# Modulation products with two k tiles of 512 outputs in a block: four column-group matmuls of 512 columns instead of sixteen of 128

## The chip, the cores and the metric

The kernel runs on one core of a Trainium2 chip (trn2). The metric is the device time of one execution in microseconds, as the median of several. The kernel uses five queues: TensorE (PE), VectorE (DVE), ScalarE (ACT), GpSimd (POOL) and SyncE (SP), which here only issues transfers.

## What is computed

Two blocks of two layers each. The first is a diffusion-style transformer block with adaptive modulation: an mLSTM and convolution mixer, then grouped attention, each followed by an MLP. The second has three attention branches. Only the modulation is touched here:

```python
silu_c = jax.nn.silu(c)          # (1, 1024)
silu_cc = jax.nn.silu(c_ctx)     # (1024,)
for layer in range(2):
    mod_x = jnp.split((silu_c @ ada_w[layer] + ada_b[layer])[:, None, :], 6, axis=-1)
    mod_c = jnp.split((silu_cc @ ada_w[layer] + ada_b[layer])[None, None, :], 6, axis=-1)
    hx = rms_norm(x, norm1_g[layer]) * (1 + mod_x[1]) + mod_x[0]
    ...
    x = x + mod_x[2] * y_x
    x = x + mod_x[5] * sqrelu_mlp(rms_norm(x, norm2_g[layer]) * (1 + mod_x[4]) + mod_x[3], ...)
```

`ada_w` is (2, 1024, 6144) in fp32: two vectors (c and c_ctx) times 12288 outputs, over 1024 inputs.

## The kernel before

**The modulation (ada).** `ada_w` is streamed as 96 blocks of 128 partitions x 1024 words (0.5 MB each). Two blocks are a pair; there are 48 pairs `q`. In the kernel before, a block holds 128 outputs with all eight k tiles of 128 inputs. `silu` holds, for each k tile, 32 columns of which two are the vectors and the rest zero. A matmul has `silu[:, k, :]` as the stationary operand (32 columns) and 128 outputs as the moving one, and writes 32 partitions of PSUM: k tile k goes to the column group k % 4, so the four groups of 32 partitions hold partial sums (`ada_products`, L1239 to L1261). The sum over the four groups, and the turn of the outputs from the free axis to partitions, are made by a second matmul in `ada_columns` (L1263 to L1270): VectorE first copies the bank to `ada_sum` (`sum_ada`, L2187), then TensorE multiplies each 128 outputs of it with `groups_to_rows`, a constant of two columns, and VectorE adds the bias and writes `mod` (`keep_ada`, L2193).

```python
for k in range(KT):
    rows = slice(32 * (k % 4), 32 * (k % 4) + 32)
    mm = pe.matmul(psum[rows, b, j * P:(j + 1) * P], silu[:, k, :], w[:, k, :], start=k < 4, stop=k >= 4)
```

**When.** The first eight pairs (16 blocks, `ADA_FIRST`) are computed at the start, since the first normalisation needs their outputs. Their blocks go through four slots of the tile `M`; SyncE loads block n when TensorE has read block n - 4 (L224 to L229), and behind the first four blocks it loads X (3 MB, both segments). VectorE adds up the squares of X between the pairs' sums (`ADA_SQUARES`, L2208 to L2216: k tiles 0 and 1 behind pair 1, and so on to pair 4). When all is done, `rms_stats` sums the squares on TensorE. The other 40 pairs are done at 40 points of the hybrid mixer's four heads, each behind a projection: `ada(point)` on TensorE (L1272) and on VectorE (L2201). Their blocks go through three slots of `stage`. In both programs a point has the columns of the pair before and then the products of its own pair; at the start the products of pair q come before the columns of pair q - 1.

**Queues.** Each engine runs its program in order. TensorE takes PSUM tiles from a ring of four banks (`Tiles.take`, waits `bank_free`); VectorE and ScalarE step through the same ring (`look`, `skip`) and wait for `tile_done`. `ada_tiles(point)` (L56) tells ScalarE how many tiles of the ring a point uses, so that it can skip them. The projections are matmuls in three terms (high and low parts of fp32r operands, L1111 to L1113, in `mm3`). ScalarE makes the high part of each weight block (L379), GpSimd the low part (L267).

Of the kernel before, what the change touches and what calls it, by code (L numbers as in the profile page):

```python
# [23 lines left out]
P = 128  # L24
D, KT = 1024, 8
# [8 lines left out]
ADA_BLOCKS = 2 * 6 * KT  # L34
# [21 lines left out]
def ada_tiles(point):  # L56


    q = ADA_FIRST // 2 + point
    return (point > 0 and q - 1 < ADA_BLOCKS // 2) + (q < ADA_BLOCKS // 2)  # L60

# [85 lines left out]
def build(nc, a, out, n_blocks, extra):  # L147
    with ExitStack() as ctx:  # L148
# [30 lines left out]
        silu = sb("silu", [P, KT, 32])  # L179
        ada_sum = sb("ada_sum", [P, 2, 2 * P])  # L180
        stage = sb("stage", [P, ADA_SLOTS, WORDS])
# [179 lines left out]
def act_program(nc, block, v, n_blocks, extra):  # L361
# [5 lines left out]
    def _(act):  # L367
# [130 lines left out]
        for k in range(KT):  # L498
            squares(k, ALL_SEGS)
        tiles.skip(ADA_FIRST)  # L500
        next_weights()
# [172 lines left out]
def attention_views(v):  # L674
# [6 lines left out]
    v_raw = M[:, 6 * SEQ:6 * SEQ + TOK]  # L681
    soft = v["ada_sum"][:, 0, :]
    root_q = [[soft[:, 20 + 16 * p + 8 * t:28 + 16 * p + 8 * t] for t in range(2)] for p in range(2)]
# [400 lines left out]
def pe_program(nc, block, v, n_blocks):  # L1084
# [6 lines left out]
    def _(pe):  # L1091
# [147 lines left out]
        def ada_products(q):  # L1239

            b = tiles.take(pe)
            for j in range(2):
# [5 lines left out]
                else:  # L1248
                    s = n % ADA_SLOTS
                    pe.wait_ge(v["stage_landed"][s], stage_landed[s].next(16))  # L1250
                    w = v["stage"][:, s]
                w = w.rearrange("p (k m) -> p k m", m=P)
                for k in range(KT):
                    rows = slice(32 * (k % 4), 32 * (k % 4) + 32)
                    mm = pe.matmul(psum[rows, b, j * P:(j + 1) * P], silu[:, k, :], w[:, k, :], start=k < 4, stop=k >= 4)
                if j == 0:
# [5 lines left out]

        def ada_columns(q):  # L1263

            b = tiles.take(pe)
            pe.wait_ge(v["ada_summed"], summed.next())
            for j in range(2):
                mm = pe.matmul(psum[:, b, 2 * j:2 * j + 2], ada_sum[:, q % 2, j * P:(j + 1) * P], v["groups_to_rows"],
                               start=True, stop=True)
            mm.then_inc(v["tile_done"], 1)  # L1270

        def ada(point):  # L1272

            if point > 0 and ADA_FIRST // 2 + point - 1 < ADA_BLOCKS // 2:
                ada_columns(ADA_FIRST // 2 + point - 1)
            if ADA_FIRST // 2 + point < ADA_BLOCKS // 2:
                ada_products(ADA_FIRST // 2 + point)

        for q in range(ADA_FIRST // 2):
            ada_products(q)  # L1280
            if q > 0:
                ada_columns(q - 1)
        ada_columns(ADA_FIRST // 2 - 1)

# [624 lines left out]
def dve_program(nc, block, v, a, out):  # L1909
# [7 lines left out]
    def _(dve):  # L1917
# [269 lines left out]
        def sum_ada(q):  # L2187
            b = look()
            cp(v["ada_sum"][:, q % 2, :], psum[:, b, 0:2 * P])
            free(b)  # L2190
            dve.sem_inc(v["ada_summed"], 1)

        def keep_ada(q):  # L2193
            b = look()
            i, m = q // 4, 2 * (q % 4)
            at = VEC["ada_b"] + 8 * i + m
            tt(mod[:, i, m:m + 2, :], psum[:, b, 0:4].rearrange("p (m c) -> p m c", c=2),
               vec[:, at:at + 2].unsqueeze(2).broadcast_to([P, 2, 2]), ALU.add)
            free(b)

        def ada(point):  # L2201
            if point > 0 and ADA_FIRST // 2 + point - 1 < ADA_BLOCKS // 2:
                keep_ada(ADA_FIRST // 2 + point - 1)
# [12 lines left out]
        keep_ada(ADA_FIRST // 2 - 1)  # L2216


# [1160 lines left out]
```

## Time and profile before

| | |
|---|---|
| median of 3 runs | 4305.46 us (4302.26, 4305.46, 4305.89) |
| span of the profiled execution | 4300.8 us (its own time isn't given apart; the span is 1.5 under the fastest run and 4.7 under the median) |
| TensorE matmul, weight load | 3983.3 us (93%), 3344.5 us (78%) |
| VectorE, ScalarE, GpSimd | 2080.8, 1500.1, 1648.3 us (48, 35, 38%) |
| ada products (L1255) | 1536 recorded passes, 7.5 to 473.4 us from the start |
| ada columns (L1268) | 192 recorded passes |

Matmul rows are passes, not matmuls: an fp32 matmul is recorded twice. A row's busy time covers its instructions from the first start to the last end, overlaps counted once, while "mean ns" is that of one, latency included; the distance from one start to the next tells the rate. Behind "idle before" stands what the engine last waited for; "DVEq L1972" is an event that VectorE's queue raised in line 1972. PEclk is the granted clock as a share of 2.4 GHz. ACT, DVE and POOL rows are single instructions on their engines.

### The profile page before, as it was taken

The page shows a single profiled execution, that of the slowest core. Times are in us where ns is not written, and L with a number is a line of the kernel's source. Part 1 is how long each engine was busy: PE and PEld are TensorE (multiplying, and loading weights), DVE is VectorE, ACT ScalarE, POOL GpSimd, SP SyncE. Part 2 cuts the span into 40 slices and gives each one's busy share as a digit, 9 for nine tenths or more (in the row PEclk, how much of TensorE's full clock was granted, in tenths as well). Part 3 has the DMA queues.
Part 4 walks back from the last instruction along what each step waited for, and adds up shares of the span by engine and source line. Part 5 has one row for each costly group of instructions (what it writes and reads, how often), then busy time and mean ns, then how long its engine had stood idle before and what let it go on. Part 6 is the DMA issues. An engine that isn't in the chain of part 4 may idle for free.

```text
span 4300.8 us, 62447 instructions
## 1 busy us (share of the span) xinstructions
PE 3983.3 (93%) x20764; PEld 3344.5 (78%) x20764; DVE 2080.8 (48%) x3374; ACT 1500.1 (35%) x2430; POOL 1648.3 (38%) x2044
## 2 busy tenths in 40 slices
PE   7899889999979889999899999899989999998997
PEld 6788779999967767887676778688866767887886
DVE  5655654322347764235737622532356475225225
ACT  2221221111235543222645633322245455333223
POOL 1111123333321115566243345465632433554655
PEclk7899989999989999999999999899989999999998
DMA  5333211111110002322121122233211211322222
GB/s 182 130 130 123 78 50 53 61 63 59 64 40 20 25 18 93 98 93 94 45 74 54 54 83 94 65 98 98 93 60 40 79 49 55 98 89 71 96 96 89
DMA packets 92774, 328.55 MB, mean 76 GB/s; under 512 B 10240, under 2 KB 12544, under 8 KB 92544
## 3 DMA queue, kind: packets, MB, share of 16 engines
q1 hardware_dynamic: 90928, 323.61, 22.8%
q8 instruction: 140, 2.29, 0.2%
q10 hardware_dynamic: 1616, 1.90, 0.1%
q14 instruction: 90, 0.74, 0.1%
HBM read 323.38 MB, written 2.10 MB: 76 GB/s over the span
## 4 chain that ended last, share of the span: by engine, by line
issue 65%; POOL 34%; POOLq 1%
POOL Wl L267 34%; POOLq L262 0%; POOLq L264 0%; POOLq L267 0%; POOLq L148 0%; POOLq L261 0%; POOLq L3371 0%
## 5 line engine op out<-in xcount | busy, mean ns | idle before, releaser
L267 POOL TENSOR_TENSOR Wl<-raw,Wh 128x256 fp32r<-128x256 f32 x2040 | 1648.1, 838 | 2651.9 <-ACT Wh L379 2651.7
L379 ACT ACTIVATE Wh<-raw 128x1024 fp32r<-128x1024 f32 x510 | 540.1, 1059 | 1748.8 <-PE psum L1113 1743.3
L1111 PE MATMUL psum<-Hh,Wh 128*128 128x512 f32 (+1 forms) x2704 | 1041.0, 385 | 72.6 <-DVEq L1972 24.7
L1112 PE MATMUL psum<-Hl,Wh 128*128 128x512 f32 (+1 forms) x2704 | 1015.9, 376 | 0.0
L1113 PE MATMUL psum<-Hh,Wl 128*128 128x512 f32 (+1 forms) x2704 | 1015.2, 375 | 0.0
L1111 PE MATMUL psum<-Gh,Wh 128*128 128x512 f32 (+3 forms) x2032 | 753.1, 371 | 27.3 <-DVEq L1972 16.3
L1113 PE MATMUL psum<-Gh,Wl 128*128 128x512 f32 (+3 forms) x2032 | 746.1, 367 | 0.0
L1112 PE MATMUL psum<-Gl,Wh 128*128 128x512 f32 (+3 forms) x2032 | 746.0, 367 | 0.0
L1111 PEld LDWEIGHTS psum<-Hh,Wh 128*128 128x128 f32 x2704 | 517.5, 191 | 198.8 <-issue 56.6
L1113 PEld LDWEIGHTS psum<-Hh,Wl 128*128 128x128 f32 x2704 | 517.3, 191 | 72.5
L1112 PEld LDWEIGHTS psum<-Hl,Wh 128*128 128x128 f32 x2704 | 518.6, 192 | 65.8 <-issue 1.9
L1111 PEld LDWEIGHTS psum<-Gh,Wh 128*128 128x128 f32 (+1 forms) x2032 | 383.7, 189 | 90.6 <-DVEq L1972 24.2
L1113 PEld LDWEIGHTS psum<-Gh,Wl 128*128 128x128 f32 (+1 forms) x2032 | 383.3, 189 | 51.9
L1112 PEld LDWEIGHTS psum<-Gl,Wh 128*128 128x128 f32 (+1 forms) x2032 | 383.9, 189 | 50.2 <-issue 1.1
L1929 DVE TENSOR_TENSOR hand<-hand 128x512 f32<-128x512 f32 (+1 forms) x160 | 111.8, 699 | 449.0 <-ACT hand L389 433.5
L2111 DVE SCALAR_TENSOR_TENSOR X<-psum,mod,X 128x256 f32<-128x256 f32 (+1 forms) x160 | 84.4, 548 | 375.1 <-PE psum L1113 374.6
L2107 DVE SCALAR_TENSOR_TENSOR X<-X,psum 128x512 f32<-128x512 f32 x64 | 44.0, 687 | 248.4 <-PE psum L1113 247.5
L2140 DVE TENSOR_TENSOR Gl<-hand,Gh 128x512 fp32r<-128x512 f32 (+1 forms) x160 | 155.5, 972 | 5.6
L1938 DVE CAST Gh<-hand 128x512 fp32r<-128x512 f32 (+1 forms) x160 | 117.7, 735 | 5.5
L1929 DVE TENSOR_TENSOR S<-psum,hand 128x512 f32<-128x512 f32 x32 | 22.1, 691 | 199.6 <-PE psum L1113 199.0
L923 ACT ACTIVATE stage<-psum,soft 128x512 f32<-128x512 f32 x128 | 86.5, 685 | 85.7 <-DVE soft L2959 85.6
L389 ACT ACTIVATE hand<-psum 128x512 f32<-128x512 f32 (+3 forms) x180 | 90.2, 525 | 9.6 <-DVEq L1975 9.6
(339 smaller groups left out, 4733.2 us busy)
## 6 DMA issues: line engine op xcount, KB each, us to landing
raw<-in_wstream SPq DMA_DIRECT2D x510, 512.0 KB, 3.4
stage<-in_ada SPq DMA_DIRECT2D x80, 512.0 KB, 4.2
M<-in_ada SPq DMA_DIRECT2D x16, 512.0 KB, 5.4
X<-in_xT SPq DMA_DIRECT2D x1, 2048.0 KB, 14.8
out<-X SPq DMA_DIRECT2D x8, 256.0 KB, 2.0
X<-in_ctxT SPq DMA_DIRECT2D x1, 1024.0 KB, 9.9
M<-in_memT ACTq DMA_DIRECT2D x1, 1024.0 KB, 5.3
M<-in_axial ACTq DMA_DIRECT2D x1, 512.0 KB, 3.6
```

What stands on the lines that cost most here:

```text
L267: last = pool.tensor_tensor(Wl[:, s, c], raw[:, s, c], Wh[:, s, c].bitcast(F32), ALU.subtract)
L379: act.activation(Wh[:, s], raw[:, s], ACT.Copy).then_inc(v["w_high"], 1)
L389: last = act.activation(hand[p, s, cols], one, func, **k)
L923: last = act.activation(stage[:, s, c * SEQ:(c + 1) * SEQ], psum[:, 4 + 2 * j + c, :], ACT.Exp, bias=soft[:, 4 * j + c:4 * j + c + 1], acc ...
L1111: pe.matmul(dst, a[0], b[0], start=first, stop=False)
L1112: pe.matmul(dst, a[0], b[1], start=False, stop=False)
L1113: return pe.matmul(dst, a[1], b[0], start=False, stop=last)
L1929: do(dve.tensor_tensor(dst, x, y, op))
L1938: do(dve.tensor_copy(dst, x))
L2107: last = dve.scalar_tensor_tensor(out=X[:, m, t0:t0 + n], in0=X[:, m, t0:t0 + n], scalar=1.0, in1=psum[:, b, 0:n], op0=ALU.mult, op1=ALU.add)
L2111: last = dve.scalar_tensor_tensor(out=X[:, m, lo:hi], in0=psum[:, b, lo - t0:hi - t0], scalar=mod[:, part, m, c:c + 1], in1=X[:, m, lo:hi] ...
L2140: do(dve.tensor_tensor(Gl[:, m, t0:t0 + w], r, Gh[:, m, t0:t0 + w].bitcast(F32), ALU.subtract))
```

## The change

A block now holds 512 outputs with two k tiles, so four blocks (two pairs) hold 512 outputs over all eight. Block j of pair q has the k tiles 4 (q % 2) + 2 j and the next, each of which goes to its own column group, as one matmul of 512 columns that fills the whole PSUM bank. VectorE copies the bank of an even pair to `ada_sum` (now one buffer of 512 columns, formerly two of 256) and adds the bank of the odd pair to it. The columns come once for two pairs, as four matmuls, and one bias instruction for 4 x 2 values. They stand before the products of the next even pair, at the start too. The points, the slots, the blocks' number and size, and the engines' other work are the same; the host packs the blocks in the new order.

```diff
-    return (point > 0 and q - 1 < ADA_BLOCKS // 2) + (q < ADA_BLOCKS // 2)
+    return len(ada_columns_at(point)) + (ADA_FIRST // 2 + point < ADA_BLOCKS // 2)
+
+
+def ada_columns_at(point):
...
     q = ADA_FIRST // 2 + point
+    return [q // 2 - 1] if point > 0 and q % 2 == 0 and q <= ADA_BLOCKS // 2 else []
...
-        ada_sum = sb("ada_sum", [P, 2, 2 * P])
+        ada_sum = sb("ada_sum", [P, 4 * P])
...
-                w = w.rearrange("p (k m) -> p k m", m=P)
-                for k in range(KT):
-                    rows = slice(32 * (k % 4), 32 * (k % 4) + 32)
-                    mm = pe.matmul(psum[rows, b, j * P:(j + 1) * P], silu[:, k, :], w[:, k, :], start=k < 4, stop=k >= 4)
+                w = w.rearrange("p (k m) -> p k m", m=4 * P)
+                for i in range(2):
+                    group = 2 * j + i
+                    k = 4 * (q % 2) + group
+                    mm = pe.matmul(psum[32 * group:32 * group + 32, b, :], silu[:, k, :], w[:, i, :], start=True, stop=True)
...
-            for j in range(2):
-                mm = pe.matmul(psum[:, b, 2 * j:2 * j + 2], ada_sum[:, q % 2, j * P:(j + 1) * P], v["groups_to_rows"],
+            for j in range(4):
+                mm = pe.matmul(psum[:, b, 2 * j:2 * j + 2], ada_sum[:, j * P:(j + 1) * P], v["groups_to_rows"],
                                start=True, stop=True)
...
         for q in range(ADA_FIRST // 2):
+            if q > 0 and q % 2 == 0:
+                ada_columns()
             ada_products(q)
-            if q > 0:
-                ada_columns(q - 1)
-        ada_columns(ADA_FIRST // 2 - 1)
+        ada_columns()
...
         def sum_ada(q):
             b = look()
-            cp(v["ada_sum"][:, q % 2, :], psum[:, b, 0:2 * P])
+            if q % 2 == 0:
+                cp(v["ada_sum"][:], psum[:, b, :])
+            else:
+                tt(v["ada_sum"][:], v["ada_sum"][:], psum[:, b, :], ALU.add)
+                dve.sem_inc(v["ada_summed"], 1)
             free(b)
-            dve.sem_inc(v["ada_summed"], 1)
...
         for q in range(ADA_FIRST // 2):
+            if q > 0 and q % 2 == 0:
+                keep_ada(q // 2 - 1)
             sum_ada(q)
-            if q > 0:
-                keep_ada(q - 1)
...
-    ada = w["ada_w"].reshape(2, KT, P, 6 * KT, P).transpose(0, 3, 2, 1, 4).reshape(ADA_BLOCKS, P, WORDS)
+    ada = w["ada_w"].reshape(2, KT // 2, 2, P, 12, 4 * P).transpose(0, 4, 1, 3, 2, 5).reshape(ADA_BLOCKS, P, WORDS)
```

The order on TensorE at the start, from the columns of the first outputs on, through pairs 2 and 3, first before the change (L1255 products, one pair is 16 matmuls; L1268 columns; `ada_landed` is a block's transfer, `ada_summed` VectorE's sum):

```order
L1268 MATMUL psum<-const,ada_sum 128x2 [waits ada_summed,bank_free2]
L1268 MATMUL psum<-const,ada_sum 128x2
L1255 MATMUL psum<-M,silu 32x128 [waits ada_landed0,bank_free3]
L1255 MATMUL psum<-M,silu 32x128 x7
L1255 MATMUL psum<-M,silu 32x128 [waits ada_landed1]
L1255 MATMUL psum<-M,silu 32x128 x7
L1268 MATMUL psum<-const,ada_sum 128x2 [waits ada_summed,bank_free0]
L1268 MATMUL psum<-const,ada_sum 128x2
L1255 MATMUL psum<-M,silu 32x128 [waits ada_landed2,bank_free1]
L1255 MATMUL psum<-M,silu 32x128 x7
L1255 MATMUL psum<-M,silu 32x128 [waits ada_landed3]
L1255 MATMUL psum<-M,silu 32x128 x7
```

And with the change (L1262 products, L1275 columns):

```order
L1275 MATMUL psum<-const,ada_sum 128x2 [waits ada_summed,bank_free2]
L1275 MATMUL psum<-const,ada_sum 128x2 x3
L1262 MATMUL psum<-M,silu 32x512 [waits ada_landed0,bank_free3]
L1262 MATMUL psum<-M,silu 32x512
L1262 MATMUL psum<-M,silu 32x512 [waits ada_landed1]
L1262 MATMUL psum<-M,silu 32x512
L1262 MATMUL psum<-M,silu 32x512 [waits ada_landed2,bank_free0]
L1262 MATMUL psum<-M,silu 32x512
L1262 MATMUL psum<-M,silu 32x512 [waits ada_landed3]
L1262 MATMUL psum<-M,silu 32x512
L1275 MATMUL psum<-const,ada_sum 128x2 [waits ada_summed,bank_free1]
L1275 MATMUL psum<-const,ada_sum 128x2 x3
```

Before, the sum waited for between two pairs was that of the pair ahead of the last one; now it is that of the last one, and comes after every second pair.

On VectorE at the same place, from the end of the squares of k tiles 0 and 1 (S sums the squares), before:

```order
L1938 COPY ada_sum<-psum 128x256 [waits v_chain,tile_done]
L1929 TENSOR_TENSOR mod<-psum,vec 128x4 [waits v_chain,tile_done]
L1929 TENSOR_TENSOR S<-S,hand 128x384 [waits v_chain,handed] x4
L1938 COPY ada_sum<-psum 128x256 [waits v_chain,tile_done]
L1929 TENSOR_TENSOR mod<-psum,vec 128x4 [waits v_chain,tile_done]
L1929 TENSOR_TENSOR S<-S,hand 128x384 [waits v_chain,handed] x4
```

And with the change:

```order
L1936 TENSOR_TENSOR mod<-psum,vec 128x8 [waits v_chain,tile_done]
L1945 COPY ada_sum<-psum 128x512 [waits v_chain,tile_done]
L1936 TENSOR_TENSOR S<-S,hand 128x384 [waits v_chain,handed] x4
L1936 TENSOR_TENSOR ada_sum<-ada_sum,psum 128x512 [waits v_chain,tile_done]
L1936 TENSOR_TENSOR S<-S,hand 128x384 [waits v_chain,handed] x4
```

The four additions of squares stood behind a sum whose columns were already in TensorE's queue behind another pair; now the second sum of a group stands behind them, with TensorE's columns waiting for it.

## Rows read from the trace of the kernel before

**Rows 1.** The page, part 1: busy time of the engines.

```profile
PE 3983.3 (93%) x20764; PEld 3344.5 (78%) x20764; DVE 2080.8 (48%) x3374; ACT 1500.1 (35%) x2430; POOL 1648.3 (38%) x2044
```

**Rows 2.** Timeline of TensorE, start: start us, us, operation, count, idle before.

```profile
20.48 2.27 PE L1255 MATMUL psum<-M,silu 128*32 128x128 f32 x32 [8.53 <-DMA M<-in_ada]
...
23.62 1.93 PE L1255 MATMUL psum<-M,silu 128*32 128x128 f32 x32
...
31.79 0.98 PE L1268 MATMUL psum<-const,ada_sum 128*128 128x2 f32 x4 [0.30 <-DVEq L2191]
...
38.58 1.87 PE L1268 MATMUL psum<-const,ada_sum 128*128 128x2 f32 x8
40.31 2.70 PE L1198 MATMUL psum<-const,S 128*128 128x1 f32 x12
```

**Rows 3.** Stretches: length, busy PE, PEld, DVE, ACT, POOL, clock, DMA, GB/s.

```profile
20.00:44.00 24.00, 21.37 (x233) 16.74 (x234) 13.28 (x32) 11.00 (x19) 4.06 (x6) 0.50 0.79 277
...
70.00:180.00 110.00, 98.50 (x812) 88.10 (x812) 61.51 (x132) 23.59 (x42) 15.42 (x20) 0.86 0.31 107
180.00:290.00 110.00, 99.39 (x861) 88.08 (x860) 68.58 (x123) 24.20 (x43) 16.61 (x22) 0.92 0.38 137
290.00:400.00 110.00, 97.53 (x856) 87.92 (x855) 68.87 (x120) 23.68 (x39) 17.49 (x23) 0.91 0.36 130
```

**Rows 4.** Waits of TensorE, 70 to 480 us: us in total, times, longest.

```profile
PE psum L1111 <- DVE Pl L2161: 18.4, 9, 5.3
...
PE psum L1111 <- DVEq L1965: 9.1, 5, 2.1
PE psum L1255 <- DVEq L1965: 1.6, 1, 1.6
```

**Rows 5.** Timeline of TensorE in narrow windows, and one group by source.

```profile
70.01 0.33 PE L1112 MATMUL psum<-Hl,Wh 128*128 128x384 f32 x1
70.18 0.34 PE L1113 MATMUL psum<-Hh,Wl 128*128 128x384 f32 x1
70.45 0.32 PE L1255 MATMUL psum<-stage,silu 128*32 128x128 f32 x4
...
70.45 0.75 PE L1255 MATMUL psum<-stage,silu 128*32 128x128 f32 x20
...
136.71 1.13 PE L1150 MATMUL psum<-M,tab 4*128 4x512 f32 x4
...
2281.68 1.02 PE L1150 MATMUL psum<-diag,const 128*128 128x512 f32 x2
...
L1150 PE MATMUL psum<-diag,const x28: 590/590/591, 2281.7 to 3623.8; 128*128 128x512 f32 x28
```

**Rows 6.** Timeline of TensorE's weight loads at the start.

```profile
21.67 0.63 PEld L1255 LDWEIGHTS psum<-M,silu 128*32 128x32 f32 x16 [0.56 <-DMA M<-in_ada]
```

**Rows 7.** Timeline of TensorE at a point of the hybrid stage.

```profile
78.93 0.58 PE L1268 MATMUL psum<-const,ada_sum 128*128 128x2 f32 x4 [0.89 <-DVEq L2191]
79.44 1.08 PE L1255 MATMUL psum<-stage,silu 128*32 128x128 f32 x32
80.45 0.33 PE L1111 MATMUL psum<-Wh,Hh 128*128 128x128 f32 x1
```

**Rows 8.** VectorE by form, 0 to 480 us: busy us, mean ns, idle before.

```profile
L1929 DVE TENSOR_TENSOR mod<-psum,vec 128x4 f32<-128x4 f32 x47 | 7.5, 160 | 39.0 <-PE psum L1268 35.8 <-DVE Vl L1929 0.9 <-PE psum L1255 0.7
...
L1929 DVE TENSOR_TENSOR tab<-psum,tab 128x512 f32<-128x512 f32 x6 | 4.1, 691 | 0.2
```

**Rows 9.** Timeline of VectorE at a point of the hybrid stage.

```profile
187.89 0.16 DVE L1929 TENSOR_TENSOR mod<-psum,vec 128x4 f32<-128x4 f32 x1
188.20 0.42 DVE L1938 COPY ada_sum<-psum 128x256 f32<-128x256 f32 x1 [0.15 <-DVE mod L1929]
188.87 3.35 DVE L2414 RECIPROCAL tab<-tab 128x512 f32<-128x512 f32 x1 [0.25 <-DVE ada_sum L1938]
```

**Rows 10.** Timeline of VectorE at the start: the squares of two k tiles.

```profile
24.04 2.67 DVE L1929 TENSOR_TENSOR S<-S,hand 128x384 f32<-128x384 f32 x4
```

More of the change, by code:

```diff
@@ L499, in _ @@
             squares(k, ALL_SEGS)
-        tiles.skip(ADA_FIRST)
+        tiles.skip(ADA_FIRST // 2 + ADA_FIRST // 4)
         next_weights()
@@ L681, in attention_views @@
     v_raw = M[:, 6 * SEQ:6 * SEQ + TOK]
-    soft = v["ada_sum"][:, 0, :]
+    soft = v["ada_sum"]
     root_q = [[soft[:, 20 + 16 * p + 8 * t:28 + 16 * p + 8 * t] for t in range(2)] for p in range(2)]
@@ L1261, in ada_products, with ada_columns @@
                     v["ada_read"].append((v["tile_done"], tiles.at))
-        def ada_columns(q):
+        def ada_columns():
             b = tiles.take(pe)
             pe.wait_ge(v["ada_summed"], summed.next())
-            for j in range(2):
-                mm = pe.matmul(psum[:, b, 2 * j:2 * j + 2], ada_sum[:, q % 2, j * P:(j + 1) * P], v["groups_to_rows"],
+            for j in range(4):
+                mm = pe.matmul(psum[:, b, 2 * j:2 * j + 2], ada_sum[:, j * P:(j + 1) * P], v["groups_to_rows"],
                                start=True, stop=True)
@@ L1272, in ada @@
         def ada(point):
-            if point > 0 and ADA_FIRST // 2 + point - 1 < ADA_BLOCKS // 2:
-                ada_columns(ADA_FIRST // 2 + point - 1)
+            for _ in ada_columns_at(point):
+                ada_columns()
             if ADA_FIRST // 2 + point < ADA_BLOCKS // 2:
@@ L1279, in _ @@
         for q in range(ADA_FIRST // 2):
+            if q > 0 and q % 2 == 0:
+                ada_columns()
             ada_products(q)
-            if q > 0:
-                ada_columns(q - 1)
-        ada_columns(ADA_FIRST // 2 - 1)
+        ada_columns()
         rms_stats(ALL_SEGS, 0)
@@ L2188, in sum_ada, with keep_ada @@
             b = look()
-            cp(v["ada_sum"][:, q % 2, :], psum[:, b, 0:2 * P])
+            if q % 2 == 0:
[3 more added lines that the diff above has]
+                dve.sem_inc(v["ada_summed"], 1)
             free(b)
-            dve.sem_inc(v["ada_summed"], 1)
-        def keep_ada(q):
+        def keep_ada(group):
             b = look()
-            i, m = q // 4, 2 * (q % 4)
+            i, m = group // 2, 4 * (group % 2)
             at = VEC["ada_b"] + 8 * i + m
-            tt(mod[:, i, m:m + 2, :], psum[:, b, 0:4].rearrange("p (m c) -> p m c", c=2),
-               vec[:, at:at + 2].unsqueeze(2).broadcast_to([P, 2, 2]), ALU.add)
+            tt(mod[:, i, m:m + 4, :], psum[:, b, 0:8].rearrange("p (m c) -> p m c", c=2),
+               vec[:, at:at + 4].unsqueeze(2).broadcast_to([P, 4, 2]), ALU.add)
             free(b)
         def ada(point):
-            if point > 0 and ADA_FIRST // 2 + point - 1 < ADA_BLOCKS // 2:
-                keep_ada(ADA_FIRST // 2 + point - 1)
+            for group in ada_columns_at(point):
+                keep_ada(group)
             if ADA_FIRST // 2 + point < ADA_BLOCKS // 2:
@@ L2215, in _ @@
         for_pe()
-        keep_ada(ADA_FIRST // 2 - 1)
+        keep_ada(ADA_FIRST // 4 - 1)
         dve.wait_ge(v["masks_loaded"], 16)
```

## The prediction

> **What bounds the kernel now.** I read the totals of the page first. TensorE is busy for 93% of the span [rows 1], so a microsecond on its queue counts wherever it isn't waiting. The modulation work (ada) lies wholly in the first 480 us of 4300.8: of its 48 pairs eight stand at the start and 40 in the hybrid stage, and a pair's 16 matmuls are recorded as 32 passes, so an fp32 matmul runs as two passes [rows 2]. Nothing after that changes, so the question is about two stretches.
>
> The first is the start, the first 40 us: TensorE works through eight pairs of blocks between block loads and VectorE's sums, at a granted clock of 0.50 of 2.4 GHz in 20 to 44 us, i.e. 1.2 GHz [rows 3]. The second is the hybrid mixer, 70 to 480 us, where 40 pairs are slipped between the projections. There TensorE is busy for about 90% of the time [rows 3]. The chief waits in that stretch are for VectorE: 18.4 us for the low parts of the probabilities (Pl, L2161) and 9.1 us for PSUM banks to be freed (L1965), with 1.6 us more of these at the ada matmuls, 10.7 in all [rows 4].
>
> How do the narrow ada matmuls run today? By windows of the timeline that end early, starting at 70.45: four passes cover 0.32 us, twenty cover 0.75 us [rows 5]. So four passes, one for each group of 32 columns, run side by side, and each of the four further waves adds 0.11 us. A pair has 32 passes, 8 waves. On the full array a 512-column fp32 matmul shows 1.02 us for its two passes [rows 5]; a single one is recorded at 0.59 us, so the second began 0.43 us after the first: 0.107 us per 128 columns. A wave of 128 columns at 0.11 us is therefore all streaming and nearly no fixed cost.
>
> **The change, part by part.**
>
> *Products.* Sixteen matmuls of 128 columns become four of 512, one per column group. Before: 8 waves x 0.11 = 0.88 us. Now: 2 waves x 0.43 = 0.86 us, if the four groups still run together. That is 0.02 us per pair, 0.8 us over 40 pairs at most. At 1.2 GHz both double: a pair took 1.93 us [rows 2] and will take the same. The number of columns per group (1024 passed per pair) hasn't changed; that is why the cut in instructions is worth so little.
> The Trainium skill ("TensorEngine Tiling (Array Packing)", section Instruction Overhead) says otherwise: about 60 cycles of overhead for each matmul. Its 60 cycles, 25 ns at 2.4 GHz, on each of six waves saved would be an estimated 0.15 us per pair and 6 us in all, and the sum below would end at 4304.7. The spacing of 0.11 against 0.107 us speaks against it.
>
> *Half-filled waves.* A block now holds two of the four groups, where it held all four. If the second block lands late, the first one's matmuls run with two groups idle, and the pair ends a full 2 x 0.85 us (1.2 GHz) after the second landing instead of 0.85. At the start block 5 lands 0.56 us late by the weight-load row at 21.67 [rows 6]. In the hybrid stage no wait for a block stands among the ada matmuls' waits [rows 4], since three slots are loaded ahead, so I cost it at nothing there.
>
> *Columns.* 48 groups of two matmuls become 24 of four, the same 96 matmuls. Warm, two take 0.51 us from start to start (78.93 to 79.44), products 1.01 (79.44 to 80.45) [rows 7]. Two points cost 2 x 1.52 = 3.04 us now, and 0.95 + 2 x 1.0 = 2.95 afterwards, to which the odd point adds a switch from the full array to 32-column groups that the columns used to cover (70.18 to 70.45 is 0.27 us where successive projection passes stand 0.17 apart [rows 5]): 0.1 us. So 3.05 against 3.04: TensorE's own work is unchanged.
>
> *VectorE.* 48 copies of 128x256 (0.42 us) become 24 copies and 24 additions of 128x512 from PSUM; the nearest row is an addition of 128x512 with one operand in PSUM, 0.691 us [rows 8]. 48 biases (0.160 us) become 24. With what lies around them, one point takes 187.89 to 188.87 = 0.98 us: 0.16 + 0.15, then 0.42 + 0.25 [rows 9]. Afterwards an even point takes 0.31 + 0.69 + 0.15 = 1.15 and an odd one 0.69 + 0.25 = 0.94, so two points 2.09 instead of 1.96. Over 20 such twos that is +2.6 us of VectorE time. VectorE alternates between waiting and being waited for; I take 1.0 us of it as on the path.
>
> *Fewer tiles.* 20 PSUM tiles fewer go through the ring of four banks in the hybrid stage, so TensorE can run further ahead. Bounds: nothing, or half of the 10.7 us of bank waits [rows 4]. Since VectorE holds the remaining ones longer, I take nothing.
>
> *The order at the start.* This is the term that matters. Before, the columns of pair q-1 stood behind the products of pair q, so the sum by VectorE had a whole pair to hide behind; even so TensorE waited 0.30 us at 31.79 [rows 2]. Now they stand ahead of the products of pairs 2, 4 and 6, and TensorE must wait for the sum of the pair that it has only just finished, with VectorE's squares (2.67 us for four additions) in between [rows 10]. Worked forward: X ends and block 4 lands as before (20.48 [rows 2]), block 5 at 21.67. Pair 2 ends at 21.67 + 1.71 + 0.2 = 23.6. VectorE sums it to 24.3 and does squares to 27.1, and only then sums pair 3 (done at 25.3): to 27.9. Columns of the first group start at 28.1 and take 1.73 (38.58 to 40.31 holds eight passes [rows 2]), to 29.9. Pair 4 runs to 31.8; VectorE: sum to 32.5, squares to 35.3, sum of pair 5 to 36.1. Columns 36.3 to 38.1, pair 6 to 40, pair 7 to 41.8 (its blocks were asked for from 31.6 on, so they are there), its sum to 42.5, four columns 42.75 to 44.5. The statistics, and all that follows, start at 44.5 instead of 40.31: **+4.2 us**. Bounds: if VectorE never held TensorE up, only the last links remain, 0.27 for the larger sum and 0.85 for columns that no longer overlap it: +1.1. If one more half-filled pair falls on the path, 6.
>
> Sum: +4.2 + 1.0 = +5.2 us. Against the execution profiled: 4300.8 + 5.2 = 4306.0 us of span. The median of the runs, 4305.46, stands 4.7 above that span (the launch around it and the spread of the runs), so **4310.7 us**.
>
> *Clock.* The mean granted clock of 0.86, 0.92 and 0.91 in 70 to 400 us means that some 68 us there (2 x 0.14 x 110, and so on) ran at 1.2 GHz [rows 3]. These stretches follow idle time of TensorE, which shifts by microseconds. A tenth more or less would be 3.4 us of time either way.
>
> **The rivals.** A measurement tells about 0.2% of this kernel from no change, 8.6 us: faster is under 4296.9, slower over 4314.1.
> 1. *The four groups no longer run together.* If passes of 512 columns overlap only two by two (each block brings two groups, with a wait between), a pair takes 4 x 0.43 = 1.71 us, 0.85 more: 34 us over 40 pairs, and some 10 at the start at half clock: 4355 us. It decides from 0.07 us more per pair. Against: two 512-column matmuls of 4 rows each, in different row tiles and with a wait each, took 1.13 us for all four passes at 136.71, hardly more than the 1.02 of one; and today's second block has its wait before the 17th pass, which the run of twenty passes crosses without a gap [rows 5]. 6 in 100.
> 2. *The start and the hybrid stage at their upper ends.* 6 + 2.6 + 3.4 = 12: 4317. It needs VectorE's additions on the path throughout; for it speaks that VectorE is what TensorE waits for [rows 4]. 18 in 100.
> 3. *Run-ahead pays.* All bank waits go (-10.7) and the clock gains 3.4, against +4.2 at the start: 4295.6, faster. For it: 20 tiles leave the ring. Against: those waits come where VectorE does reciprocals of 3.35 us [rows 9], which no ring of four hides. 7 in 100.
> 4. *A fixed cost per matmul* that the spacing hides: at most 6 us back, 4305, no change. 10 in 100.
>
> **How the numbers follow.** The forecast has 59 in 100. Within 0.2%: 0.59 + 0.10 = 0.69; slower: 0.18 + 0.06 = 0.24; faster: 0.07. The range takes in the unknown costs: low end 1.1 - 5.3 - 3.4 = -7.6, high end rival 2, +12, and a little beyond its middle: 4299 to 4319.
>
> **What would show it.** Right: passes of the products x8 in about 1.05 us warm; columns in groups of 8 passes, 24 of them; in 20 to 44 us TensorE waits for the sum's event (28, 36 and 42 us) and the statistics start near 44.5; VectorE additions of 128x512 into ada_sum at 0.69 us; the same gap of some 5 us at 480 us as at 70. Wrong: a pair over 1.2 us warm (rival 1), the statistics before 42 us (the start was not bound by VectorE), or a gap at 480 us that differs by more than 4 us from the gap at 70.

## The result, and the profile after

The changed kernel takes **4313.8 us** (median of 17 runs, 4307.96 to 4319.96), the kernel before, in runs alternating with it on the same chip, 4305.46 us (17 runs). The ratio is 1.0019, 95% interval 1.0013 to 1.0025: slower by 8.3 us. The forecast was 4310.7 in a range of 4299 to 4319, with "no change that can be measured" as the likeliest: by the forecast's own bound for a change, 8.6 us, the 8.3 still fall under it, though the interval leaves out 1. The execution profiled took 4309.77 us, 1.8 more than its span of 4308.0.

The page, part 1, of the changed kernel, against [rows 1]:

```profile
PE 3989.0 (93%) x19612; PEld 3310.2 (77%) x19612; DVE 2093.8 (49%) x3350; ACT 1501.4 (35%) x2430; POOL 1646.8 (38%) x2044
```

TensorE has 1152 passes less (48 pairs by 24) and 5.7 us *more* busy time, VectorE 13 us more. Cutting the number of passes saved nothing. A pair at full clock, and the projection pass that follows it (timeline of TensorE, hybrid stage; columns as in [rows 2]):

```profile
82.36 1.07 PE L1262 MATMUL psum<-stage,silu 128*32 128x512 f32 x8
83.36 0.33 PE L1117 MATMUL psum<-Wh,Hh 128*128 128x128 f32 x1
```

Start to start it is 1.00 us, where it was 1.01 [rows 7]. The four groups still run side by side.

The start, timeline of TensorE, against [rows 2]:

```profile
20.78 5.54 PE L1262 MATMUL psum<-M,silu 128*32 128x512 f32 x16 [6.05 <-DMA M<-in_ada]
28.47 1.02 PE L1275 MATMUL psum<-const,ada_sum 128*128 128x2 f32 x8 [2.16 <-DVEq L2200]
29.43 3.85 PE L1262 MATMUL psum<-M,silu 128*32 128x512 f32 x16
36.62 1.84 PE L1275 MATMUL psum<-const,ada_sum 128*128 128x2 f32 x8 [3.34 <-DVEq L2200]
38.38 4.15 PE L1262 MATMUL psum<-M,silu 128*32 128x512 f32 x16
43.47 1.02 PE L1275 MATMUL psum<-const,ada_sum 128*128 128x2 f32 x8 [0.94 <-DVEq L2200]
44.35 1.48 PE L1204 MATMUL psum<-const,S 128*128 128x1 f32 x12
...
53.65 0.66 PE L1117 MATMUL psum<-Hh,Wh 128*128 128x384 f32 x1 [4.15 <-DVEq L1979]
```

Columns stand at 28.5, 36.6 and 43.5 us, each behind a wait for VectorE's sum, and the statistics begin at 44.35 instead of 40.31. But they take 1.48 us, where they took 2.70: the first projection starts at 53.65, and before at

```profile
50.83 0.66 PE L1111 MATMUL psum<-Hh,Wh 128*128 128x384 f32 x1 [4.15 <-DVEq L1972]
```

so **2.8 us** of the 4.0 are left there. The stretches tell why, against [rows 3]:

```profile
20.00:44.00 24.00, 16.79 (x69) 5.55 (x70) 13.18 (x25) 9.59 (x17) 1.02 (x2) 0.66 0.78 275
44.00:70.00 26.00, 17.44 (x83) 14.70 (x83) 19.56 (x38) 11.24 (x20) 4.49 (x7) 0.87 0.27 104
70.00:180.00 110.00, 99.98 (x569) 82.84 (x567) 65.46 (x129) 24.18 (x43) 16.55 (x20) 0.86 0.30 106
180.00:290.00 110.00, 97.41 (x585) 79.30 (x585) 71.68 (x116) 23.87 (x40) 18.15 (x24) 0.92 0.38 134
290.00:400.00 110.00, 97.25 (x593) 79.85 (x592) 71.84 (x117) 22.55 (x38) 15.31 (x20) 0.91 0.37 130
400.00:490.00 90.00, 83.04 (x513) 68.82 (x512) 58.86 (x96) 19.92 (x35) 15.34 (x20) 0.94 0.35 123
```

The granted clock in 20 to 44 us is 0.66 of 2.4 GHz, where it was 0.50; in 44 to 70 us 0.87, where it was 0.79.

The end of the hybrid stage is told by the last columns, the last place of the modulation work. The row by tile (first and last start) of before, and of the changed kernel:

```profile
L1268 PE MATMUL psum<-const,ada_sum x160: 166/251/353, 78.9 to 480.2; 128*128 128x2 f32 x160
```

```profile
L1275 PE MATMUL psum<-const,ada_sum x160: 166/251/251, 94.1 to 490.0; 128*128 128x2 f32 x160
```

They stand **9.8 us** later, of which 2.8 came from the start: 7.0 us arose in the hybrid stage, where 1.0 was forecast. After that the gap stays between 9.3 and 10.6 us to 850 us, is 8.0 at 900, and 7.2 at the end (spans of 4308.0 and 4300.8). These 2.6 us came back where the work is the same, by less idle time of TensorE; what shortened it was not looked into. Waits of TensorE, 70 to 490 us, against [rows 4]:

```profile
PE psum L1117 <- DVE Pl L2168: 19.4, 9, 5.5
PE psum L1156 <- DVEq L1979: 11.2, 7, 2.2
PE psum L1117 <- DVEq L1972: 7.8, 5, 2.1
PE psum L1262 <- DVEq L1972: 3.3, 3, 1.1
```

In all 41.7 us. Before, the same view adds 9.6 (L1150) and 1.3 (L1268) to the rows shown, 40.0 in all. So the waits explain some 2 of the 7 us. The stage as a whole, from 70 us before and 72.8 after (the same place of the program) to the last columns, of before and of the changed kernel (columns as in [rows 3]):

```profile
70.00:480.20 410.20, 369.99 (x3199) 331.07 (x3198) 254.43 (x472) 88.45 (x153) 62.94 (x81) 0.91 0.36 126
```

```profile
72.80:490.00 417.20, 374.88 (x2239) 308.01 (x2238) 265.18 (x452) 88.89 (x154) 62.98 (x81) 0.91 0.35 124
```

TensorE is busy 4.9 us longer and idle 2.1 us longer. Laid over the stretches of granted clock in the two traces, its busy time at 1.2 GHz is 64.1 us, where it was 55.2. Work at 1.2 GHz takes about twice its time (a pair 1.93 us for 1.00), so half of the 8.9 us more, 4.5, is the clock's share. Of the 7.0 us, 4.5 are thus the clock, 2.1 waits and 0.4 TensorE's own work. The mean clock, 0.91 in both, hides this: it counts idle time too.

VectorE's work by form, 0 to 490 us:

```profile
L1945 DVE COPY ada_sum<-psum 128x512 f32<-128x512 f32 x24 | 16.6, 692 | 16.5 <-PE psum L1262 15.3 <-DVE mod L1936 0.9
L1936 DVE TENSOR_TENSOR ada_sum<-ada_sum,psum 128x512 f32<-128x512 f32 x24 | 16.5, 688 | 30.0 <-PE psum L1262 29.1
...
L1936 DVE TENSOR_TENSOR mod<-psum,vec 128x8 f32<-128x8 f32 x23 | 3.8, 167 | 20.0 <-PE psum L1275 18.9 <-DVE Vl L1936 0.5
```

These are the durations that the forecast took (0.69, 0.69, 0.16).

### The profile page after: what moved, and what is told of

Its sections match the earlier page's. It is cut to its first block, busy times and chain, and to the rows that moved or that the text cites. A ratio compares the mean times of both kernels' runs of the same rounds, so it can differ in the third digit from the quotient of the medians.

```text
span 4308.0 us, 60047 instructions
## 1 busy us (share of the span) xinstructions
PE 3989.0 (93%) x19612; PEld 3310.2 (77%) x19612; DVE 2093.8 (49%) x3350; ACT 1501.4 (35%) x2430; POOL 1646.8 (38%) x2044
## 4 chain that ended last, share of the span: by engine, by line
issue 65%; POOL 34%; POOLq 1%
POOL Wl L273 34%; POOLq L268 0%; POOLq L270 0%; POOLq L273 0%; POOLq L154 0%; POOLq L267 0%; POOLq L3381 0%
```

## The experiments

Three theories for the 7 us of the hybrid stage. **A**: VectorE's longer sums. **B**: the late start, which shifts everything behind it against the clock's stretches. **C**: TensorE's own order, that is the columns of two old pairs standing together at every second point.

All results first. "Start" is the gap to the kernel before at the first projection (50.83), "hybrid end" that at the last columns (480.2), both in the profiled execution; the median's difference is against the kernel before in the same set of runs (4304.7 to 4306.5). A gap is that of one execution against one, and both can lie off their kernel's median: the one of the kernel before took 4302.26 us, 3.2 under it, that of fill_pairs 6.6 over its own, that of new_start 5.0 under. Small differences between gaps need the medians beside them. The ratio is not quite the quotient of the medians; the fit further down goes by the ratios. Where an expectation counts blocks, they are the weight blocks as ScalarE rounds them: in the kernel before, block 9 is at 210 us, blocks 20 to 23 at 435 to 489.

| kernel | median | against before | ratio, 95% interval | start | hybrid end |
|---|---|---|---|---|---|
| the change | 4313.8 | +8.3 | 1.0019 (1.0013 to 1.0025) | 2.8 | 9.8 |
| old_start | 4312.54 | +7.1 | 1.0012 (1.0003 to 1.0021) | 1.2 | 10.4 |
| new_start | 4309.41 | +4.0 | 1.0011 (1.0002 to 1.0020) | 3.3 | 4.0 |
| late_3 | 4306.48 | +1.1 | 1.0006 (0.9998 to 1.0015) | 4.9 | 3.4 |
| short_sums | 4305.3 | -0.1 | 0.9998 (0.9989 to 1.0007) | 3.1 | 1.2 |
| wide_copies | 4317.41 | +12.7 | 1.0030 (1.0019 to 1.0041) | 0.0 | 12.7 |
| squares_moved | 4308.5 | +3.8 | 1.0010 (1.0001 to 1.0019) | 0.6 | 10.1 |
| products_first | 4312.52 | +7.8 | 1.0014 (1.0005 to 1.0023) | 2.7 | 12.3 |
| same_load | 4310.68 | +4.5 | 1.0017 (1.0008 to 1.0026) | 1.2 | 10.2 |
| two_pairs | 4307.64 | +1.4 | 1.0004 (0.9995 to 1.0013) | -0.1 | 6.2 |
| fill_change | 4312.66 | +6.2 | 1.0016 (1.0007 to 1.0026) | 2.2 | 9.4 |
| fill_pairs | 4306.51 | 0.0 | 1.0002 (0.9993 to 1.0011) | 1.5 | 8.1 |
| odd_points | 4341.75 | +35.3 | 1.0085 (1.0071 to 1.0099) | 1.2 | 40.0 |

### Which half costs: old_start and new_start

The first has the start of the kernel before (its blocks, order and sums for the first 16 blocks) and the hybrid stage of the change; the second the reverse. In old_start:

```
-        for q in range(ADA_FIRST // 2):
-            if q > 0 and q % 2 == 0:
-                ada_columns()
-            ada_products(q)
-        ada_columns()
+        for q in range(ADA_FIRST // 2):
+            ada_products(q)
+            if q > 0:
+                ada_columns_old(q - 1)
+        ada_columns_old(ADA_FIRST // 2 - 1)
```

> The start (the first eight pairs, their block layout, sums and columns) as in the kernel before, the hybrid stage's 40 pairs as in the change. If the two parts add up, the start returns its 3 us (the statistics at 40.3 us instead of 44.4 in the trace) and what is left is the hybrid stage's own share. Theory A (the hybrid form itself costs, through VectorE's sums or through more stretches at 1.2 GHz): about 5 to 6 us over the kernel before, so 4311. Theory B (the late start shifts TensorE against the chip's clock decisions, and that made the rest): back to the kernel before within 2 us, 4305 to 4307.

> The start as in the change, the hybrid stage's 40 pairs as in the kernel before. Theory A: 3 us over the kernel before, 4308.5, and the distance between the two traces stays at 3 us through the hybrid stage. Theory B: the whole 8 us, 4313, with the distance growing in the hybrid stage.

Both halves cost: 1.0012 and 1.0011, which add up to the 1.0019 of the whole within their intervals. In new_start the gap stays between 3.9 and 5.0 us from 66 to 700 us, but for 6 us near 77 where it touches 5.9; nothing is added in an unchanged hybrid stage. In old_start the hybrid stage adds 9 us to a start that is 1.2 late.

### Is it only that everything is late: late_3

The kernel before, with one reciprocal of 512 columns more on VectorE ahead of the statistics:

```
+        do(dve.reciprocal(diag.rearrange("p b q -> p (b q)"), const_cols))
```

> The kernel before with one more reciprocal of 512 columns on VectorE (3.35 us, into a tile that nothing reads then) before it lets TensorE start the statistics. A pure delay of about 3 us at 40 us. Theory A: 3 us over the kernel before, 4308.5. Theory B: as the change, 4313, since only the delay matters.

The gap is 4.9 us at the first projection and 3.4 at the last columns, and the median is within the interval of no change. Theory B falls: a late start alone doesn't come out larger at the end of the stage.

### VectorE's sums: short_sums and wide_copies

The change with sums of 128 columns in the hybrid stage (it leaves out three quarters of the hybrid stage's sums, so most of the modulation):

```
-                cp(v["ada_sum"][:], psum[:, b, :])
+                cp(v["ada_sum"][:, cols], psum[:, b, cols])
```

> The change, but in the hybrid stage VectorE copies and adds only the first 128 of the 512 columns (the others keep their sums of the start, so most of the modulation there is left out): 0.29 us instead of 0.69 for each of 40 sums, 16 us less work for VectorE. If VectorE's longer sums made the hybrid stage's share, it goes, and some more: 4308 or less. If it is the clock through something else, the time stays at 4312 to 4314.

And the kernel before with each copy of the hybrid stage done twice:

```
             cp(v["ada_sum"][:, q % 2, :], psum[:, b, 0:2 * P])
+            if q >= ADA_FIRST // 2:
+                cp(v["ada_sum"][:, q % 2, :], psum[:, b, 0:2 * P])
```

> The kernel before, in which VectorE does each copy of a pair's sum in the hybrid stage twice: 0.42 us more per point, 40 points, about 17 us more work of VectorE with nothing else moved. It measures how much of VectorE's added work comes out as time. Theory A (VectorE's longer operations carry the hybrid share of the change, because VectorE is late at its reciprocals): half of it or more shows, 8 to 17 us at 490 us, so 4313 to 4322. Theory C (the hybrid share comes from TensorE's side, the order of its wide passes and columns, and VectorE has room): the gap at 490 us stays under 4 us and the time at or under 4309. Late in the hybrid stage the gap then either stays or shrinks with the clock, by some 3 us.

The two copies are recorded at 0.88 us where one took 0.42 [rows 9]: 0.46 us more at 40 points, 18.4 in all, of which 12.7 come out: **0.7 us for each us of VectorE's work** in this stage. Short sums take 16 us off VectorE (40 sums of 0.69 down to 0.29), and the gap at the hybrid end falls by 8.6 us. So VectorE's time matters here, and Theory A looked proven. It wasn't: the change adds only 2.6 us of such work, worth 1.8. The price was right and the quantity too small by far; that sent me to the next pair.

### The same VectorE load, TensorE's order kept: same_load and two_pairs

same_load is the change with copies of 384 columns (it leaves out a quarter of what they copy), so that two points cost VectorE what they cost before:

```
+            n = 4 * P if q < ADA_FIRST // 2 else 3 * P
             if q % 2 == 0:
-                cp(v["ada_sum"][:], psum[:, b, :])
+                cp(v["ada_sum"][:, 0:n], psum[:, b, 0:n])
```

> The change, in which the copies of the hybrid stage carry 384 of the 512 columns (it leaves out a quarter of what they copy, so a part of the modulation). A copy then takes some 0.56 instead of 0.69 us, and two points hold VectorE for 1.96 us, exactly as in the kernel before: what is left of the change in the hybrid stage is TensorE's order of work, its wide passes and its tiles. Theory A (VectorE's 2.6 us of added work carry the hybrid share): the gap to the kernel before at 490 us falls from 9.8 us (the change) to 3 to 4.5 us, and the median comes to 4306 to 4309. Theory A', by the slope of 0.6 to 0.7 us per us of VectorE's work which two other runs gave: 1.7 us less, a gap of 8. Theory C (TensorE's order, with its new waits for a bank ahead of the products and the stretches at 1.2 GHz behind them): the gap stays at 8 to 10 us and the median at 4311 to 4314.

two_pairs is the kernel before with nothing but the grouping taken over: products of 128 columns, copies of 256, and the columns of two pairs at every second point, with one bias for both:

```
-    return (point > 0 and q - 1 < ADA_BLOCKS // 2) + (q < ADA_BLOCKS // 2)
+    return len(ada_columns_at(point)) + (q < ADA_BLOCKS // 2)
...
-            if point > 0 and ADA_FIRST // 2 + point - 1 < ADA_BLOCKS // 2:
-                ada_columns(ADA_FIRST // 2 + point - 1)
+            for q in ada_columns_at(point):
+                ada_columns(q, 2)
```

> The kernel before with its own start, products and copies, in which the columns of two pairs stand together at every second point of the hybrid stage, as in the change: one bank and one bias of 128x8 for two pairs. VectorE does 20 biases of 0.16 us with 0.15 us around each less, 6.2 us in all, and 20 tiles fewer go through the ring. If VectorE's work sets the hybrid share at 0.6 to 0.7 us per us, the gap to the kernel before at 490 us is -4 us, the median 4300 to 4302: a version that beats both. Theory C (the order of the change's hybrid stage costs by itself, whatever VectorE does): the gap is 0 to +5 us and the median 4305 to 4310.

Theory A falls as the whole explanation. With VectorE's load as before, the gap is still 10.2 us (1.2 of it from the start), where A asked for 3 to 4.5. With 6.2 us *less* than before, and the products as they were, it is 6.2 us and the median 4307.64, where A asked for -4 and 4300 to 4302. C stands, less firmly than the gaps suggest: the median of two_pairs is only 1.4 us over the kernel before, within the interval of no change, and what shows a price of the grouped order is that the 6.2 us of saved work don't come out (the fit below). The Trainium skill ("TensorEngine Tiling (Array Packing)", section PSUM Bottleneck) advises to combine PSUM accesses to tiles of one bank into one; two_pairs does that with its biases; VectorE's work falls by these 6.2 us, and the time does not.

Where two_pairs loses time can be read to the place. Timeline of TensorE in two_pairs:

```profile
200.02 0.95 PE L1277 MATMUL psum<-const,ada_sum 128*128 128x2 f32 x8
202.06 1.08 PE L1262 MATMUL psum<-stage,silu 128*32 128x128 f32 x32 [1.09 <-DVEq L1974]
204.94 0.69 PE L1118 MATMUL psum<-Hh,Wh 128*128 128x384 f32 x1 [1.80 <-DVEq L1974]
205.42 0.53 PE L1119 MATMUL psum<-Hl,Wh 128*128 128x384 f32 x1
```

and at the same place of the program in the kernel before:

```profile
202.36 0.50 PE L1268 MATMUL psum<-const,ada_sum 128*128 128x2 f32 x4
202.94 1.08 PE L1255 MATMUL psum<-stage,silu 128*32 128x128 f32 x32
205.82 0.45 PE L1111 MATMUL psum<-Hh,Wh 128*128 128x384 f32 x1 [1.80 <-DVEq L1965]
206.10 0.34 PE L1112 MATMUL psum<-Hl,Wh 128*128 128x384 f32 x1
```

At 204.94 two_pairs is 0.88 us *ahead*. Then its projection passes stand 0.32 us apart, those of before 0.175. The stretches behind, of two_pairs and of before (columns as in [rows 3]):

```profile
204.00:210.60 6.60, 5.66 (x18) 5.66 (x19) 5.55 (x12) 0.53 (x1) 0.00 (x0) 0.50 0.40 153
```

```profile
206.00:211.00 5.00, 4.81 (x32) 4.50 (x32) 4.24 (x10) 0.86 (x2) 0.00 (x0) 1.00 0.30 120
```

Clock 0.50 against 1.00: 17 passes at 1.2 GHz, each 0.15 us longer, 2.5 us lost, and the kernel is 1.6 behind at 210.54 where it had been 0.88 ahead (0.9 at the next products, since it has no columns there). The kernel before has its stretch at 1.2 GHz some 10 us earlier in the program, over four transposes (195.30, 2.93 us) and one projection pass. There it costs hardly anything: two_pairs runs these transposes at full clock and is 2.3 us ahead at 198 us, and by 204 only 0.9, since it then waits 1.09 us for a bank that VectorE has not freed. Time lost ahead of a wait for VectorE is taken out of the wait; time lost on the projections behind it is kept.

Counted from 180 to 211 us and from 420 to 480 us (times of the kernel before), the gap grows by 1.9 and 4.4 us in the change and in two_pairs, by 1.2 and 3.2 in short_sums, and by nothing in new_start. It is tempting to lay these steps to the grouped order, but two kernels without it have them too: late_3 (1.7 and 2.6) and wide_copies (2.1 and 6.3). late_3 gives back 5.1 us between them, from 211 to 420 us, where the change gives back nothing. So the clock's share of the 7 us is read from the trace, but that the grouped order as such brings these steps on is not shown.

### Can the place be mended: fill_change, fill_pairs, odd_points

The first two do the columns twice at the three points with the 1.1 us wait ahead of the products (205, 328, 451 us), so that TensorE works where it idled:

```
-                ada_columns()
+                ada_columns(2 if point in (12, 24, 36) else 1)
```

> The change, in which the four columns matmuls of three points of the hybrid stage (those where TensorE waited 1.1 us for a bank ahead of the products, at 205, 328 and 451 us) are done twice: 0.95 us of work for TensorE in place of that wait, nothing added elsewhere. Theory D (the idle time that the grouped order gathers there, 1.1 us ahead of the products and 1.8 behind them, is what brings on the stretches at 1.2 GHz on the projections behind it, 207 to 214 and 453 to 460 us): those stretches go or move to cheaper work, the steps of 2 us at block 9 and of 4 us at blocks 20 to 23 go, and the gap at 490 us falls from 9.8 to 3 to 5 us. Theory E (the stretches fall by where earlier ones ended and not by this wait, or the steps are not the clock's): the gap stays at 9 to 10 us.

> The kernel with the columns of two pairs together and the products and copies of the kernel before, in which the columns of the same three points are done twice. Theory D: the gap to the kernel before at 490 us falls from 6.2 us to 0 or below (-1 to 1 us), the median to 4300 to 4304. Theory E: it stays at 5.5 to 6.5 us.

Theory D falls: the gaps are 9.4 and 8.1 us, the latter with 1.5 from the start. The wait ahead of the products goes from 3.3 to 0.6 us in all, and the stretch at 1.2 GHz stays where it was:

```profile
202.90 1.84 PE L1275 MATMUL psum<-const,ada_sum 128*128 128x2 f32 x16
204.94 1.06 PE L1262 MATMUL psum<-stage,silu 128*32 128x512 f32 x8 [0.20 <-DVEq L1972]
207.82 0.69 PE L1117 MATMUL psum<-Hh,Wh 128*128 128x384 f32 x1 [1.81 <-DVEq L1972]
208.31 0.52 PE L1118 MATMUL psum<-Hl,Wh 128*128 128x384 f32 x1
```

What moves the stretch is not settled by this: not that wait.

odd_points is two_pairs with the double columns at the odd points:

```
-    return [q - 2] if point > 0 and q % 2 == 0 and q <= ADA_BLOCKS // 2 else []
+    if point == 1 or q == ADA_BLOCKS // 2:
+        return [(q - 1, 1)]
+    return [(q - 2, 2)] if point > 1 and q % 2 and q < ADA_BLOCKS // 2 else []
```

> The kernel before with its own start, products and copies, the columns of two pairs together at every second point as before, but at the odd points of the hybrid stage in place of the even ones, so that the double columns no longer stand at the three points where VectorE's reciprocals hold the banks (12, 24 and 36). Theory D (it is the place of the double columns that costs): no wait of 1.1 us ahead of products at 203, 325 and 448 us, and the gap at 490 us is -4 to +1 us, the median 4300 to 4305. Theory C as first put (the grouped order costs wherever it stands): the gap is 5 to 7 us, as with the even points.

Neither: 4341.75 us, by far the slowest. Up to 210 us all went as hoped; the kernel was 5.1 us ahead of the one before. Then one wait, in its timeline of TensorE, and the stretches from there on and behind:

```profile
204.83 0.34 PE L1122 MATMUL psum<-Hh,Wl 128*128 128x384 f32 x1
208.36 1.84 PE L1279 MATMUL psum<-const,ada_sum 128*128 128x2 f32 x8 [3.19 <-DVEq L2202]
210.13 1.93 PE L1264 MATMUL psum<-stage,silu 128*32 128x128 f32 x32
```

```profile
208.00:255.80 47.80, 46.29 (x276) 43.74 (x277) 16.44 (x33) 3.03 (x4) 4.64 (x7) 0.50 0.26 89
260.00:280.00 20.00, 17.79 (x156) 14.94 (x154) 10.29 (x22) 2.99 (x6) 2.80 (x4) 0.99 0.48 182
```

Columns at an odd point need the sum of the point just before it, and that copy (207.63 on VectorE) stood behind the second of two reciprocals (200.85, 2.55 us) and nine operations more. TensorE idled 3.19 us, the clock fell, and it stayed at 1.2 GHz for 48 us although TensorE was busy for 46.29 of the 47.80. The gap went from -5.1 to +17.9 us. The same came again at 348 us, and took it from 12.3 to 35.7.

### The start: squares_moved and products_first

squares_moved is the change with VectorE's squares behind the sums that close a group:

```
-ADA_SQUARES = ((), (0, 1), (2, 3), (4, 5), (6, 7), (), (), ())
+ADA_SQUARES = ((), (0, 1), (), (2, 3, 4, 5), (), (6, 7), (), ())
```

> The change, in which VectorE's squares at the start stand behind the sums that close a group and not behind the ones that open it, so that a group's second sum isn't held up: the columns no longer wait for 2.67 us of squares, and the whole of the statistics' squares comes in fewer places. If the waits at the sums are what costs the start (the theory of the prediction), the statistics start 2 to 3 us earlier than in the change, at 41.5 to 42.5 us, and the gap to the kernel before stays 2 to 3 us smaller through the hybrid stage. Rival: the start's time is set by the blocks' landing and by the clock, and what is saved there is lost to a stretch at 1.2 GHz: the statistics start at 43 to 44.5 us and the gap stays.

The statistics start at 42.06 and the first projection at 51.46, 2.2 us earlier than in the change, as expected. The median is 5.3 us under the change's (another set of runs; 1.0010 and 1.0019, intervals that overlap). In the profiled execution the gap at the hybrid end is 10.1 all the same: the trace agrees with the first half of the theory only.

products_first puts the products of a pair ahead of the columns, with a second buffer for sums:

```
         for q in range(ADA_FIRST // 2):
-            if q > 0 and q % 2 == 0:
-                ada_columns()
             ada_products(q)
+            if q > 0 and q % 2 == 0:
+                ada_columns((ada_sum, diag_sum)[(q // 2 - 1) % 2])
```

> The change, in which the products of a pair stand ahead of the columns of the last group at the start, as in the kernel before, with a second buffer for the sums. TensorE then has a whole pair to do while VectorE adds up. By the prediction's working the statistics start within 1.5 us of the kernel before (40.3 to 41.8 us), the hybrid share stays as the change has it (some 6 us at 490 us), and the time is near 4311 (as with the start of the kernel before and the hybrid stage of the change, 4312.5). Rival: the hybrid share depends on when it starts, and the time comes out at 4307 or less.

The waits for sums shrink (0.47 and 0.60 us), and yet the statistics start at 43.81, only 0.5 us sooner than in the change. Timeline of TensorE:

```profile
29.89 1.02 PE L1277 MATMUL psum<-const,diag 128*128 128x2 f32 x8 [0.47 <-DVEq L2226]
31.53 1.47 PE L1262 MATMUL psum<-M,silu 128*32 128x512 f32 x4 [0.61 <-DMA M<-in_ada]
33.22 4.21 PE L1262 MATMUL psum<-M,silu 128*32 128x512 f32 x12 [0.22 <-DMA M<-in_ada]
38.03 1.02 PE L1277 MATMUL psum<-const,ada_sum 128*128 128x2 f32 x8 [0.60 <-DVEq L2226]
38.98 1.05 PE L1262 MATMUL psum<-M,silu 128*32 128x512 f32 x4
40.94 1.05 PE L1262 MATMUL psum<-M,silu 128*32 128x512 f32 x4 [0.90 <-DMA M<-in_ada]
```

TensorE now waits for blocks, three times, and a pair falls apart into x4 and x4: the half-filled waves that the forecast priced for block 5 alone. The waits for sums had covered them. My expectation (within 1.5 us of the kernel before) failed. Two things seem to hold the start, each hidden behind the other. How much of it is the order is open, though, for waits for blocks come and go between executions of one start: that of the kernel before has none behind 24 us in its own trace, 0.64 and 1.21 us in old_start, 1.66 and 1.28 in odd_points.

### Three prices from seven medians

If the parts add, the median's differences are sums of a start s, a grouped order g, and v for each us of VectorE's work in the hybrid stage (+2.6 in the change and old_start, -13.4 in short_sums, +18.4 in wide_copies, -6.2 in two_pairs, 0 in same_load). Taking each kernel's ratio minus 1 times 4305 (8.2, 5.2, 4.7, -0.9, 12.9, 7.3, 1.7) and fitting by least squares with the intervals as weights: s = 3.4, g = 3.9, v = 0.62, which give 8.9, 5.5, 3.4, -1.1, 11.4, 7.3 and 0.0 for the change, old_start, new_start, short_sums, wide_copies, same_load and two_pairs. None is off by more than 1.7 us, where each interval reaches 2.6 to 4.7 to a side; s and g themselves are known to some 2.5 us, v to 0.2. Without g the best fit gives -3.6 for two_pairs, 5.3 under what was measured, and 1.5 for old_start, 3.7 under. The two fill kernels, which the fit didn't use, should be 8.9 and 0.0 and are 6.9 and 0.9 by their ratios. In the change, old_start, short_sums and same_load g takes in the wide products as well; only two_pairs and fill_pairs have the grouping alone. It is a fit, worked out behind the runs; odd_points shows that it ends where a long wait comes in.

## Why the prediction was right and wrong

**Products.** Right: 1.00 us for 1.01, nothing gained from 1152 passes less. Rival 1 (groups two by two, 1.71) falls with it, and rival 4 as well. The Trainium skill ("TensorEngine Tiling (Array Packing)", section Instruction Overhead) would have had 0.15 us saved per pair by its 60 cycles, an estimate; the trace, with 0.01 us, doesn't agree.

**Half-filled waves.** Right for the hybrid stage (no wait for a block). At the start products_first has more of them than the one forecast; in the change they stay hidden behind the waits for sums.

**Columns.** TensorE's own time for two points is as worked out. What the sum left out is where they stand: the step "20 PSUM tiles fewer ... I take nothing" and the columns' "unchanged" treated the grouped order as free. It costs 3.9 ± 2.4 us by the fit, and two_pairs, with 6.2 us less VectorE work, is no faster than the kernel before. This is the step that failed. What the grouped order does to cost this is not known.

**VectorE.** The quantity was right (durations to 0.01 us), and of 2.6 us (busy time and the fixed time around it) I took 1.0 as on the path; by v it is 1.6.

**The order at the start.** The mechanism was right, place by place: columns forecast at 28.1, 36.3 and 42.75 us came at 28.5, 36.6 and 43.5, the statistics forecast at 44.5 at 44.35. The size was 2.8 to 3.4 instead of 4.2, since the clock gave some back: I had reckoned all of the start at 1.2 GHz, as before, and the statistics ran in 1.48 us instead of 2.70. That 44.35 agrees so well is luck in part: the last columns stood 0.7 us later than forecast and took 0.88 us instead of 1.73. Nor is one pair of traces the measure. In the table, six executions with the start of the kernel before have a gap of -0.1 to 1.5 us at the first projection (0.6 in the mean; late_3 left out), five with the changed one 1.2 to 3.3 (2.5): 1.9 us apart.

**Clock.** I had a term of ±3.4 us for it and no sign. The trace of the change has its stretches at 1.2 GHz on projections at 208 and 453 us, where the kernel before has them on transposes or not at all. My test at 480 us said so: "a gap at 480 us that differs by more than 4 us from the gap at 70" was to prove the forecast wrong, and it does differ, 9.8 against 2.8.

**Sum.** Forecast 4.2 + 1.0 = 5.2; by the fit 3.4 + 3.9 + 1.6 = 8.9; measured 8.3. The range held it, since rival 2 (start and hybrid stage at their upper ends, 4317) was in it. (By the forecast's own low end, 7.6 us under 4305.46, the range should begin at 4298, not 4299.) By size the result lies halfway between the forecast, 3.1 us below it, and that rival, 3.2 above; by cause it is neither, since rival 2 put the rest on VectorE's additions. That it lies so near the forecast is helped by the start, which cost less than was put down for it. Rival 3 (run-ahead pays) falls: the wait ahead of products went from 1.6 to 3.3 us.

**What stays open.** Why the grouped order costs, and what moves the stretches. It is not the wait ahead of the products (fill_change, fill_pairs). Nor does it take the grouped order: wide_copies and late_3, both without it, show both steps. It may be that the kernel before merely has them in a good place, and that whatever shifts TensorE by a microsecond or two against VectorE there gives that up. No run tests this, and each kernel has one trace only. And no version beat the kernel before: two_pairs and fill_pairs can't be told from it.

## What to carry to other kernels

Count columns passed, not instructions: matmuls that already follow each other at their streaming rate give nothing back when they are merged. Merging the small work around them is not free either, because it moves work among the places where the engines meet; look for the place where the merged piece now follows a long operation of the engine that feeds it, and price the wait there with the clock that it may cost, before counting what it saves. When a removed wait doesn't show in the time, look for the second one that it covered.

## What the runs showed of the hardware

- TensorE can stay at 1.2 GHz while it is busy: 48 us from 208 us on in odd_points, 46.29 of 47.80 us busy, around and after one wait of 3.19 us. Over each of two such stretches the gap grew by 23 us, far more than by the wait in it.
- More idle time didn't mean a lower clock. In 20 to 44 us the kernel before was busy for 21.37 us and granted 0.50, the change for 16.79 and granted 0.66.
- Filling an idle 0.9 us with repeated matmuls left the stretch at 1.2 GHz where it was (207.8 us on in fill_change, 208.4 in the change).
- Four matmuls of 512 columns in four column groups cost no less than sixteen of 128: 1.00 and 1.01 us per pair.
- A stretch at 1.2 GHz ahead of a wait for VectorE cost hardly anything (four transposes at 195 us in the kernel before), one on 17 projection passes behind it 2.5 us (two_pairs, 205 us).
